# Merging a head norm with the next preparation, loading scan masks once, and moving one product in the scan

## The reference, cut to what matters

```python
def rwkv7_prepare(pa, prm):
    ...
    w_raw = prm['w0'] + jnp.einsum('bsdl,dlc->bsdc', jnp.tanh(wl), prm['w2'])
    decay = jnp.exp(-jnp.exp(-jax.nn.softplus(-w_raw) - 0.5))
    iclr = jax.nn.sigmoid(prm['a0'] + jnp.einsum('bsdl,dlc->bsdc', al, prm['a2']))
    g = jax.nn.sigmoid(gl) @ prm['g2']
    kk = (k * prm['k_k']).reshape(bn, s, A_HEADS_2, HEAD_DIM)
    kk = kk / jnp.maximum(jnp.sqrt(jnp.sum(kk * kk, axis=-1, keepdims=True)), 1e-12)
    k_dir = k[:, :, None, :] * (1 + (iclr - 1) * prm['k_a'])
    ...
def step(state, inp):
    r_t, w_t, k_t, v_t, kk_t, a_t = inp
    sa = jnp.einsum('bhvk,bhk->bhv', state, -kk_t)
    state = (state * w_t[:, :, None, :] + sa[..., None] * (kk_t * a_t)[:, :, None, :]
             + v_t[..., None] * k_t[:, :, None, :])
    return state, jnp.einsum('bhvk,bhk->bhv', state, r_t)

def rwkv7_output(f, y, prm, dtype):
    mu = jnp.mean(y, axis=-1, keepdims=True)
    var = jnp.mean(jnp.square(y - mu), axis=-1, keepdims=True)
    yn = ((y - mu) * lax.rsqrt(var + GN_EPS)).reshape(bn, s, A_WIDTH_2) * prm['gn_w'] + prm['gn_b']
    bonus = jnp.sum(f['r'][:, :, None] * f['k'] * prm['r_k'], axis=(2, 4))
    yn = yn + (bonus[..., None] * f['v']).reshape(bn, s, A_WIDTH_2)
    return (yn * f['g']).astype(dtype)
```

## Time and profile before

| | us |
|---|---|
| median of 3 runs (3544.7 to 3545.88) | 3545.79 |
| profiled execution, its own time | 3539.18 |
| its span, first to last instruction | 3537.4 |
| PE / DVE / ACT / POOL busy in the span | 3202.2 / 2208.1 / 1298.0 / 146.5 |

### The profile page before, as it was taken

How to read it: one execution, slowest core, us unless ns; L and a number is a source line. 1 busy time by engine, 2 the same in 40 slices (tenths; PEclk the granted TensorE clock), 3 DMA queues, 4 the chain that set the end, 5 groups by cost and what they waited for, 6 DMA issues and landing times. The chain is left out here.

```text
span 3537.4 us, 53773 instructions
## 1 busy us (share of the span) xinstructions
PE 3202.2 (91%) x21886; PEld 2573.6 (73%) x21886; DVE 2208.1 (62%) x3940; ACT 1298.0 (37%) x2245; POOL 146.5 (4%) x222
## 2 busy tenths in 40 slices
PE   6989999997899969987887989998999998889999
PEld 5768877655788758865665867887887876678777
DVE  7678866696788675667555637554666336653344
ACT  2343333324433333245534534222233335642243
POOL 0300000200000000000211100000000000000000
PEclk9989999999999989998898989999999999999999
DMA  7424553112233422120000022333232121022221
GB/s 303 168 101 179 190 179 113 61 36 66 97 140 135 143 102 85 60 89 12 20 33 11 4 85 108 119 119 108 107 143 107 54 98 59 1 78 96 81 104 60
DMA packets 64773, 340.78 MB, mean 96 GB/s; under 512 B 15120, under 2 KB 16656, under 8 KB 29072
## 3 DMA queue, kind: packets, MB, share of 16 engines
q1 hardware_dynamic: 61616, 325.51, 26.2%
q0 software_dynamic: 2048, 9.48, 0.8%
q10 hardware_dynamic: 864, 2.36, 0.2%
HBM read 326.53 MB, written 10.79 MB: 95 GB/s over the span
## 5 line engine op out<-in xcount | busy, mean ns | idle before, releaser
L265 DVE TENSOR_TENSOR weight_lo<-weight_ring,weight_hi 128x1024 fp32r<-128x1024 f32 x341 | 423.1, 1242 | 170.2 <-ACT weight_hi L250 165.1
L250 ACT CAST weight_hi<-weight_ring 128x1024 fp32r<-128x1024 f32 x341 | 356.0, 1044 | 158.0 <-PE banks L422 91.9
L420 PE MATMUL banks<-hT_hi.1,weight_hi 128*128 128x512 f32 x896 | 365.7, 408 | 25.5 <-PEq L383 23.5
L421 PE MATMUL banks<-hT_lo.1,weight_hi 128*128 128x512 f32 x896 | 358.8, 400 | 0.0
L422 PE MATMUL banks<-hT_hi.1,weight_lo 128*128 128x512 f32 x896 | 358.5, 400 | 0.0
L420 PEld LDWEIGHTS banks<-hT_hi.1,weight_hi 128*128 128x128 f32 x896 | 171.4, 191 | 68.7 <-issue 26.4
L422 PEld LDWEIGHTS banks<-hT_hi.1,weight_lo 128*128 128x128 f32 x896 | 171.1, 191 | 41.9
L421 PEld LDWEIGHTS banks<-hT_lo.1,weight_hi 128*128 128x128 f32 x896 | 171.3, 191 | 41.5 <-issue 1.9
L420 PE MATMUL banks<-hT_hi.3,weight_hi 128*128 128x512 f32 (+1 forms) x512 | 174.6, 341 | 0.0
L422 PE MATMUL banks<-hT_hi.3,weight_lo 128*128 128x512 f32 (+1 forms) x512 | 173.3, 338 | 0.0
L421 PE MATMUL banks<-hT_lo.3,weight_hi 128*128 128x512 f32 (+1 forms) x512 | 173.1, 338 | 0.0
(11 more groups left out here) (746 smaller groups left out, 7324.1 us busy)
## 6 DMA issues: line engine op xcount, KB each, us to landing
weight_ring<-ff SPq DMA_DIRECT2D x64, 1024.0 KB, 5.0
weight_ring<-ada SPq DMA_DIRECT2D x48, 1024.0 KB, 4.8
weight_ring<-up SPq DMA_DIRECT2D x44, 1024.0 KB, 6.9
weight_ring<-ada_ffn SPq DMA_DIRECT2D x24, 1024.0 KB, 4.9
weight_ring<-down SPq DMA_DIRECT2D x20, 1024.0 KB, 4.9
weight_ring<-ada_mix SPq DMA_DIRECT2D x16, 1024.0 KB, 4.8
first_blocks.1<-ada_mix SPq DMA_DIRECT2D x8, 1024.0 KB, 11.9
weight_ring<-cv_in SPq DMA_DIRECT2D x8, 1024.0 KB, 4.8
```

The source lines that it names most:

```text
L250: self.nc.scalar.copy(hi, raw).then_inc(self.hi_made, 1)
L265: self.nc.vector.tensor_tensor(lo, raw, hi.bitcast(F32), ALU.subtract).then_inc(self.lo_made, 1)
L420: nc.tensor.matmul(out, w_hi, x_hi, start=first, stop=False)
L421: nc.tensor.matmul(out, w_hi, x_lo, start=False, stop=False)
```

## The change

1. `head_norm_stage` is called for half two only. The head norm of half one is done inside `prepare_stage` of half two, whose parameter `norm` is true there. Its steps are put between those of the preparation, on each engine. r and v are brought back in that block.
2. In both preparations the spread of the keys' inverses and the keys' normalization come before the first w product. The w product of all rounds uses banks 4 and 5, the a product banks 6 and 7. b is made for each round right after k_dir.
3. The masks are loaded and cast once, in the preparation of half one, and kept through both scans. The scan's waits for them go. POOL's zeroing of S and y goes behind the decay products of chunk 0 and chunk 1; the waits for the zeroing stand at the first use of S (z from state, new state) and of y (`add_y`).
4. In the scan's loop on PE `z_from_chunk(now)` comes after `g_x(now, 5)` and `g_x(new, 2)`.

`a_product(i)` is built like `w_product(i)`, with banks 6 and 7, and waits for `kk_normed` 4 in round 0 and for `a_sig` after it. `spread_y(f)` waits until y is centred and for `inv_ready` f + 1, and fills banks 2f and 2f + 1; `gates(f)` waits for the first scaling of tile f (`fronted`) and uses the same banks. On DVE `scale_y(f)` is four instructions (two multiplications by the spread inverse, two with the norm's weight and `mixT`), `gate_y(f)` two. Where the diff leaves out lines on DVE there are: y's centring, the two steps on y's sums (`var_ready`), the keys times their spread inverse (`kk_normed`), two reciprocals (`inv_ready`), the totals, and bonus times v at the end, all as in the old functions.

The diff, cut to its core:

```diff
@@ recurrence
+            masks = (sb("mask_before", [P, 2, CH]), sb("masks_by_feature", [P, 2, 4, CH]), sb("unit_squares", [P, CH]),
+                     sb("level_masks", [P, LEVELS, 2, CH], U8))
             for half in range(2):
-                head_norm_stage(half, rcols, lora, r, y, v, mixT, flat)
+                if half == 1:
+                    head_norm_stage(half, rcols, lora, y, mixT, flat)
@@ prepare_stage, sync (after w2, a2 and reset)
+                    if masks is not None:
+                        before, by_feature, unit, _ = masks
+                        sp.dma_start(level_f32, dram["level_masks"]).then_inc(masks_loaded, 16)
+                        sp.dma_start(before[:], dram["mask_before"]).then_inc(masks_loaded, 16)
+                        sp.dma_start(by_feature[:], dram["masks_by_feature"][:, 0:2]).then_inc(masks_loaded, 16)
+                        sp.dma_start(unit[:], dram["unit_squares"]).then_inc(masks_loaded, 16)
+                        sp.wait_ge(masks_loaded, 64)
+                    if norm:
+                        sp.dma_start(g2[:], dram["g2"][half - 1]).then_inc(g_loaded, 16)
+                        sp.dma_start(flat_of(r), parked_rkv[:, 0:2 * TOK]).then_inc(brought, 16)
+                        sp.dma_start(flat_of(v), parked_rkv[:, 4 * TOK:6 * TOK]).then_inc(brought, 16)
+                        sp.wait_ge(brought, 32)
@@ prepare_stage, tensor
+                    def w_product(i):
+                        if i == 0:
+                            pe.wait_ge(kk_normed, 2)
+                        else:
+                            pe.wait_ge(w_sig, 2 * i)
+                        for s, seg in enumerate(HALVES):
+                            nc.tensor.matmul(ps[4 + s][:, 0:width[s]], w2[:, d, f * P:(f + 1) * P], lora[:, 0, seg],
+                                             start=True, stop=True).then_inc(w_mm, 1)
...
+                    if norm:
+                        for i, (f, s) in enumerate(jobs):
+                            nc.tensor.matmul(ps[i][:, 0:width[s]], head_ones[:], y[:, f, HALVES[s]], start=True, stop=True).then_inc(mean_mm, 1)
                     for f in range(2):
                         pe.wait_ge(kk_sq, f + 1)
                         sums_by_token(ps[7][:, f * 2 * TOK_T:(f + 1) * 2 * TOK_T], tmp[:, f, :]).then_inc(kk_sums, 1)
+                    if norm:
+                        for f in range(2):
+                            pe.wait_ge(squared, 2 * f + 2)
+                            sums_by_token(ps[6][:, f * 2 * TOK_T:(f + 1) * 2 * TOK_T], y_squares[:, f, :]).then_inc(var_sums, 1)
+                    pe.wait_ge(kk_inverse, 1)
+                    spread_to_features(ps[4:6], by_token[:, 0, :]).then_inc(kk_spread, 1)
+                    if norm:
+                        pe.wait_ge(var_ready, 2)
+                    spread_to_features(ps[6:8], by_token[:, 1, :]).then_inc(kk_spread, 1)
+                    if norm:
+                        spread_y(0)
                     pe.wait_ge(loaded, 48)
+                    w_product(0)
+                    a_product(0)
+                    if norm:
+                        spread_y(1)
+                    w_product(1)
+                    a_product(1)
+                    if norm:
+                        pe.wait_ge(g_loaded, 16)
+                        gates(0)
+                        gates(1)
+                    for i in range(2, 4):
+                        w_product(i)
+                        a_product(i)
@@ prepare_stage, scalar (between the keys' squares and their root; after their root)
+                    if norm:
+                        for i, (f, s) in enumerate(jobs):
+                            act.wait_ge(centred, i + 1)
+                            nc.scalar.activation(y_squares[:, f, HALVES[s]], y[:, f, HALVES[s]], ACT.Square).then_inc(squared, 1)
...
+                    if norm:
+                        for f in range(2):
+                            act.wait_ge(var_ready, f + 1)
+                            nc.scalar.activation(y_by_token[:, f, :], y_by_token[:, f, :], ACT.Sqrt).then_inc(root_ready, 1)
@@ prepare_stage, vector (after the keys' inverse)
+                    if norm:
+                        dve.wait_ge(var_sums, 2)
...
+                    else:
+                        dve.wait_ge(masks_loaded, 64)
+                        nc.vector.tensor_copy(masks[3][:].rearrange("p l d n -> p (l d n)"), level_f32).then_inc(levels_cast, 1)
                     for f in range(2):
                         dve.wait_ge(kk_spread, f + 1)
...
+                    if norm:
...
+                    if norm:
+                        scale_y(0)
+                    scan(0)
+                    if norm:
+                        scale_y(1)
+                    scan(1)
+                    finish_kdir_and_b(0)
+                    if norm:
+                        gate_y(0)
+                    scan(2)
+                    finish_kdir_and_b(1)
+                    if norm:
+                        gate_y(1)
+                    scan(3)
...
+                    finish_kdir_and_b(2)
+                    bonus(0)
+                    from_the_end(2)
+                    finish_kdir_and_b(3)
+                    bonus(1)
+                    from_the_end(3)
...
@@ scan_stage: the loads, DVE's cast and the waits before each engine's loop go; gpsimd
-                    for x in (S[0], y[:]):
-                        nc.gpsimd.memset(x, 0.0).then_inc(zeroed, 1)
+                    decay_bk(0)
+                    nc.gpsimd.memset(S[0], 0.0).then_inc(zeroed, 1)
+                    gather_v(0)
+                    decay_bk(1)
+                    nc.gpsimd.memset(y[:], 0.0).then_inc(zeroed, 1)
+                    gather_v(1)
@@ scan_stage, tensor
                         if has_now:
-                            z_from_chunk(now)
                             g_x(now, 5)
                         if has_new:
                             g_x(new, 2)
+                        if has_now:
+                            z_from_chunk(now)
                         if coming < NCH:
                             a(coming)
```

190 lines of the change are left out of this document (105 added, 85 removed).

## The result

The kernel before took 3545.25 us (median of four runs, 3544.7 to 3545.88), the changed one 3522.91 (median of four, 3520.17 to 3525.63): ratio 0.9937 with a 95% interval of 0.992 to 0.9954, 22.3 us less. The profiled execution of the changed kernel took 3525.63 us, with a span of 3523.8. The median is thus what was forecast (3523.0), but the parts are not, as the blocks show.

The account below looks back on a forecast made before the run. The prediction took the recurrence's blocks, run one after another with barriers, as the bound, so time saved in any comes off the end. Its terms, +2.1 - 8.4 - 8.2 - 8.3 = -22.8 us, gave 3523.0 us, range 3517 to 3534.

Parts of the forecast that it names:

- Part 1: Preparation of half one: keys' norm before the w product delays the first DVE scan; block 2.1 us longer, bounds +1 to +5.
- Part 2: Start of each scan: no wait for masks, PE's products start earlier; 4.2 us less per scan, 8.4 in all.
- The prediction's 1.1 us: Scan start: by the skill's exclusion rule, four DVE instructions could hold POOL for 1.1 us, cutting the 8.4 gain to 6.4.
- Part 3: Scan chunks: z's first part fills PE's 0.43 us hole before the a product; 4.1 us less per scan, 8.2 in all.
- Rival (a): Scan chunks: z's move gives nothing because another wait replaces the hole; sum -14.6, 3531.2 us; chance 0.16 shared with another rival.
- Part 4: Head norm one and preparation two merged: 51.6 us against 59.91, 8.3 less; bounds 5 to 10.5.
- The clock in the scans' fill: PE's clock rise after each scan's start: no term in the sum, only plus or minus 1 us per scan.
- The base: Whole kernel: profiled execution of 3539.18 us, counterpart 3516.4, carried to a median 6.6 us higher, giving 3523.0.
- The bounds: Whole kernel: the terms' bounds were said to add up to -31 and -4 us.
- Rival (c): PE at half clock: no change if only in preparations (chance 0.06), slower, up to 3571 us, if lasting into scans (0.04).

Follow-up runs that it names:

- after_no_z: The changed kernel with z's first part put back ahead of the inverse products: 3527.05 us, ratio 0.9958 to the kernel before.
- before_again: The kernel before, unchanged, run once more for a second trace: 3543.94 us.
- after_again: The changed kernel, unchanged, run again: 3519.9 us, ratio 0.9934 to the kernel before.
- masks_only: The kernel before with only the masks loaded and cast in preparation one and POOL's zeroing behind the first decays: 3532.74 us, ratio 0.9962.
- warm_all: The changed kernel with idle PE products in both preparations' tails and in each scan's fill: 3509.06 us, ratio 0.9909 to the kernel before.
- z_only: The kernel before with only z's first part moved behind the two inverse products: 3535.0 us, ratio 0.9977.
- blocks_only: The kernel before with only the merged block and the norms-first order in preparation one: 3534.23 us, ratio 0.9971.
- order_only: The kernel before with the norms-first order in both preparations, head norm one still its own block: 3540.77 us, ratio 0.9996.
- before_warm: The kernel before with idle PE products in preparation tails and scan fills, plus sixteen ahead of each scan's mask wait: 3540.49 us, ratio 0.9996.
- warm_tails: The changed kernel with twelve idle PE products in each preparation's tail: 3520.08 us, ratio 0.9936 to the kernel before.
- fill_only: The changed kernel with eleven idle 128x256 PE products in each scan's fill, none elsewhere: 3508.77 us, ratio 0.9907 to the kernel before.

## Why the forecast was right, and where it wasn't

The time, 3522.91 us, lies on the forecast. The four edits did what was worked out, but the account behind the sum has two errors, the clock in the fills and the base, which cancelled. That the median lies within 0.1 us of 3523.0 is luck; that the kernel gains some 20 us is not.

- **Part 1** (+2.1): right, +2.0. The first DVE scan starts 16.71 us after the block's start (forecast 16.85). The masks came later than forecast: the cast waited 0.77 us for them and began 8.7 us after the block's start (forecast: loads there near 7). It still ended, at 9.3, before the first spread did, at 10.9, and so cost nothing.
- **Part 2** (-4.2 per scan): right. The second set of the factors comes 1.51 us after the first instead of 6.04, the third 6.82 later instead of 6.48: 4.2 us. The row chosen for POOL beside DVE held as well: the b products took 1.12 us (forecast from 1.06), so one pair lost 0.26. The prediction's 1.1 us, worked out by the Trainium skill ("SBUF — State Buffer", "Who interferes with whom"), is not what the trace shows for POOL. But DVE paid as well: beside POOL its second product by the factors took 0.45 us and the two behind it 0.75, against 0.29 for the first one and 0.49 for the same two in the kernel before. These rows don't rule out that the two engines took turns, instruction by instruction; what it cost is within the 4.2 us measured.
- **Part 3** (-4.1 per scan): right. The hole is gone, and after the fill the first scan is 4.4 us and the second 3.4 us shorter; after_no_z, the other way round, gives 4.8 and 4.0. The second scan has less because the clock went to half once more just before its end, for 3.4 us from 2021.43 on: up to 136 us after their start the two scans run within 0.2 us of each other, and at their end they are 1.2 apart. Rival (a) is out.
- **Part 4** (-8.3): right in kind, 1.0 too small. The first scan in it starts 22.30 us after the block's start (forecast 22.85); the sums took 7.13 us (granted clock 0.74) instead of 8.75, and ended 11.1 us in, not 11.6, though they began a microsecond late. Against before_again the block wins 7.3 us, so the size of this gain is known to some 2 us only. From its first scan on DVE had no idle time worth naming, as forecast.
- **The clock in the scans' fill**: put at nothing in the sum, with plus or minus 1 per scan in part 2's bounds, and this is the term that was wrong. In the changed kernel it costs 3.1 us in the two steps behind the third set of factors and 0.2 to 0.4 in the next. The two scans gave 5.3 + 4.1 = 9.4 us instead of 16.6.
- **The base**: the sum was taken from one execution of before at 3539.18 and carried over to a median 6.6 us above it, as if both kernels stood as far from their medians. In two executions the recurrence takes 417.95 us before and 401.16 after, 16.8 less, and the medians differ by 22.3. before_again shows part of the rest: the kernel before has the slow fill in some scans (recurrence 422.13 us, 20.9 to 21.0 more than after and after_again), so its median already holds a part of what the changed kernel pays in all four scans. The rest is larger than what single traces can place: outside the recurrence, where no edit lies, the spans hold 3119.5 and 3120.0 us in the two executions before, and 3122.6 and 3116.9 in the two of the changed kernel. The recurrence starts anywhere between 1639.0 and 1647.0 us, though nothing ahead of it differs.
- **The bounds**: the terms' bounds on the slow side add up to 5 - 2 x 2.7 - 0 - 5 = -5.4, not -4 as the prediction has it. The stated range doesn't hang on it.

Rival (c), half clock to the slower side, named the right mechanism at the wrong place and size. Neither preparation block stayed at half, but the fills did, for 8 us more. Its price of 6.6 us for a cold chunk is that of a full chunk; in the fill PE has less to do, and 8 us more at half clock cost 3.3. What the Trainium skill says in "TensorE: Matmul & The Clock Gate", section "HAM oscillation — how this bites in real kernels" (repeated waits keep the array at half rate), agrees with the fill in part: PE was busy 19.54 of 25.20 us there, waiting between groups, and the clock stayed at half. But the fill had waits before the change too, and there the clock rose after 17 us with less work done (8.04 of 16.97 us), and in masks_only it rose after the very same work and waits that the changed kernel has.

Whether the three edits' single gains add up can't be told. By the ratios they are 8.1 + 13.5 + 10.3 = 31.9 us, with some 7 us of uncertainty, against the change's 22 with some 6. By the medians they are 6.7 + 8.9 + 7.4 = 23.0 us, and nothing is missing. What the experiments do show is the clock's price within the changed kernel: a warm fill gives back 11 us by the medians, and by the traces the two scans of warm_all are 5.8 and 7.1 us shorter than those of the changed kernel. Not shown is why the clock rises later in the changed kernel. It was 13 us after the scan's start in both scans of masks_only, 17 in the profiled execution of before and one scan of z_only, 18 to 19 in blocks_only, order_only and one scan of before_again, 25 to 26 in the changed kernel, with z's move and without, and 30 in one scan each of z_only and before_again. The masks' edit alone has the early rise and the blocks' edit alone leaves it at 18; the late one stands in every scan that has both edits and no idle products. z's place doesn't decide it; more than that stays open.

## What to carry to other kernels

Read the granted clock at the start of each stage before and after a change that brings the stage forward: the steps of the fill (here 7.90 and 5.05 us against 5.49 and 3.99 at full clock) tell at once whether a gain was given back. Where PE's first rounds in a stage are thin, a few idle products put exactly where it waits can be worth more than an edit (here 11 us); put where they delayed the first real product, in before_warm, they cost as much as they gave. And price a change against several executions of the kernel before, since one of them may be lucky by as much as a term of the sum (here 4.2 us of recurrence between two executions of the kernel before).

## What was not expected of the hardware

- Idle products ahead of a stage needn't keep the clock up in it: in warm_tails it fell 2 us into the first scan and stood at half for 24 us more, with PE busy 20.35 of 26.01 us. In fill_only and warm_all, with eleven 128x256 products in the fill itself, it was full through the fill of three of four scans, and through all but 3.4 us of the fourth.
- The same scan of the same kernel took 148.7 and 152.8 us in two executions, with the clock rising 17 and 30 us after its start.
- Two scans with the same first 12.87 us (PE busy 8.24 and 8.21 us, clock 0.50) had their clock rise 13 and 25 us after the start, in masks_only and in the changed kernel.
- DVE and POOL beside each other: the pair of POOL products took 1.12 us beside DVE and 0.86 to 0.92 otherwise, and the pair of DVE products beside them took 0.75 us where it had taken 0.49.
